# Small-block products of the gate and up projections: one weight row chunk at a time in place of two, with the raw rows released one chunk sooner

## The chip, the cores and the metric

The kernel runs on one core of a Trainium2 chip, as one launch. The metric is the device time of that core in microseconds (us), as the median of several runs. The engines of the core are TensorE (PE; its weight loads are listed apart as PEld), VectorE (DVE), ScalarE (ACT), GpSimd (POOL) and SyncE (SP), which issues most of the DMAs.

## The reference

One layer of an encoder on 1024 tokens of width 1024 in float32. First a mixer (gated short convolution and neighbourhood attention), then a mixture of experts, in which nearly all of the time studied here is spent:

```
logits = h @ w_router + b_router                     # 32 experts
top_v, top_i = top_k(logits, 4); gates = softmax(top_v)
# for each expert e, with xb the tokens that chose it:
g = minimum(xb @ w_gate[e] + b_gate[e], 7)
u = clip(xb @ w_up[e] + b_up[e], -7, 7)
y = (g * sigmoid(1.702 * g) * (u + 1)) @ w_down[e] + b_down[e]
out[token] += gate * y                               # plus the residual
```

w_gate, w_up and w_down are 1024 x 1024 float32 for each of 32 experts: 12 MB an expert, each read once from HBM.

## The kernel before

The expert part goes by passes. A pass serves one expert and up to 160 of its tokens: a main block of 128 tokens, and a small block of up to 32 more, which a pass has only if its expert was chosen by more than 128 tokens (flags `hb` for the pass whose down projection runs, `hbn` for the next pass, whose gate/up runs in the same trip of the loop).

The weights of a pass come in 12 chunks of 1 MB: 8 chunks of gate/up (chunk k holds row block k of w_gate and of w_up, 128 x 2048) and 4 of down (two row blocks each). SP loads them in order into `ring`, which has NSLOT = 6 slots; chunk c goes to slot c % 6. `room` (L463 and L464) lets SP load chunk c0 only when TensorE has finished chunk c0 - 6, which it learns from the semaphore `g_chunk` (one count for each chunk, given by the last product of the chunk). SP waits in order: a load that waits holds all later loads, the two bias loads among them (L455, L459).

For each chunk ScalarE makes w_hi, the weights rounded to a shorter float32 form (`round_weights`, L749), and VectorE makes w_lo, the raw weights minus w_hi (`rest_of_weights`, L1113). Both have six buffers. The main block's product is then three products with the 128 x 128 stationary operand x: w_hi with x_hi, w_lo with x_hi and w_hi with x_lo (`product`, L1491 to L1493), in the banks 0 to 3 of PSUM. A gate/up chunk has 4 x 3 = 12 such instructions of 512 columns.

The small block is multiplied in plain float32 straight from the raw rows in `ring` (L1502 for gate/up, L1537 for down). The output row of 1024 is cut into four quarters, and each quarter j is a product with a stationary operand of 128 x 32, whose result lies in the 32 partitions 32 j to 32 j + 31 of bank 6 (gate/up) or bank 7 (down). For one chunk k of gate/up these are four products of 512 columns, which the trace shows as 8 instructions, since a plain float32 product is two of them. The products of one or two chunks that stand together, ahead of the main products of a chunk, are called a group here.

In the loop, trip p runs on TensorE: `gate_up(p, 8, 0, ())` for chunk 0 of pass p + 1 with no small block, chunks 1 to 3 in a branch on `hbn` (`gate_up_first`), the transposes of the activations of pass p (`act_transpose`, L1525 and L1527), chunks 4 to 7 in a second branch (`gate_up_rest`), the bias rows (L1513, L1516), then the four chunks of down of pass p (`down_all`) with the transposes of pass p + 2's tokens (L1484) and its row numbers (L1474) between them, and the bias of down (L1549, L1551). The first gate/up, ahead of the loop, already does the small block chunk by chunk.

`extra_of(k, b)` says whose small-block products stand in chunk k: before, those of k - 1 and k in an odd chunk, none in an even one. So the raw rows of an even gate/up chunk are still read in the next chunk, and PAIRED lists the chunks of which `room` therefore asks for one count more. In its numbering 8, 10 and 12 are the gate/up chunks k = 0, 2 and 4 of the same trip, and 2 is k = 6 of the trip before. This holds for every pass, whether it has a small block or not, because SP's wait is the same in both.

Order on VectorE in a trip: w_lo of k = 0 and 1, the SwiGLU products of pass p (L1140 to L1145), w_lo of k = 2 and 3, slot numbers, w_lo of k = 4 and 5, aT_lo (L1150), w_lo of k = 6, 7 and of down 0 and 1, the reading of the gate and up results (`evacuate`, L1130 to L1135), w_lo of down 2 and 3, xT_lo (L1118), row numbers (L1095 to L1107).

Of the kernel before, what the change touches and what calls it, by code (L numbers as in the profile page):

```python
# [61 lines left out]
CH = 2048  # L62
NSLOT = 6
SPLIT = 6
PAIRED = (2, 8, 10, 12)
QD = 256
QT = 32
MSLOT = 4
# [44 lines left out]
def build(nc, A, out):  # L113
    ctx = ExitStack()
    with ctx:
# [252 lines left out]
        def hold(e, s, value):  # L368

            e.wait_ge(s, value)  # L370
            e.sem_inc(held, 1)
# [5 lines left out]
        def _(e):  # L377
# [83 lines left out]
            def room(p, c0):  # L461

                c = c0 - NSLOT  # L463
                hold(e, g_chunk, 12 * p + (c + 1 + (c in PAIRED)))  # L464
            e.wait_ge(e_mm, 2 * TT)
# [788 lines left out]
        def _(e):  # L1254
# [223 lines left out]
            def rows_transpose(n, first):  # L1478
                e.wait_ge(g_gat, 16 * n + 16)
                e.wait_ge(g_gatb, 16 * n + 16)  # L1480
                if not first:
                    e.wait_ge(g_ev, 2 * n)
                for k in range(KT):
                    e.transpose(bank[k // 4][:, P * (k % 4):P * (k % 4) + P], xg[:, P * k:P * k + P], ident[:, :])  # L1484
                for i in range(2):
                    ins = e.transpose(bank[2][:, P * i:P * i + P], xgb[:, P * i:P * i + P], ident[:, :])
                ins.then_inc(g_xtr, 1)
# [64 lines left out]

            def extra_of(k, b):

                return (k - 1, k) if b and k % 2 else ()
            rows_transpose(0, True)
            e.wait_ge(table_ok, 1)
            n_loop = e.value_load(table[0:1, 2 * NT:2 * NT + 1], min_val=1, max_val=MAX_PASSES)
# [18 lines left out]
            with e.Fori(0, n_loop) as p:  # L1577
# [8 lines left out]
                def gate_up_first(b):  # L1586
                    for k in range(1, 4):
                        gate_up(p, 8 + k, k, extra_of(k, b))

                def gate_up_rest(b):  # L1590
                    for k in range(4, GU_CHUNKS):
                        gate_up(p, 8 + k, k, extra_of(k, b))
                    gate_up_bias(p + 1, b)
# [55 lines left out]
```

## Time and profile before

| what | value |
|---|---|
| median of 3 runs | 2400.2 us (2400.07 to 2400.8) |
| the profiled execution, its own time | 2398.68 us |
| its span, first to last instruction | 2396.6 us |
| mean granted TensorE clock | 0.985 of full speed |
| PE busy | 2304.0 us, 96% of the span, 11110 instructions |
| PE weight loads busy | 1478.2 us, 62% |
| DVE busy | 1446.0 us, 60% |
| ACT busy | 1040.0 us, 43% |
| POOL busy | 912.5 us, 38% |
| HBM read / written | 468.34 MB / 32.05 MB |

The expert part runs from about 885 us to the end. In a line of grouped instructions the columns are: line of the kernel, engine, operation, output<-inputs, shapes, count, then busy time and mean ns of one, then idle time of the engine ahead of them with what ended it. In a timeline the first number is the start and the second the length, both in us; a bracket gives the idle time of the engine before it and what ended it ("issue" where the profile shows nothing that was waited for). A matmul's length includes the time its result takes to come out, so consecutive matmuls overlap in the rows: the distance of the starts is what one costs.

### The profile page before, as it was taken

The numbers are of one execution on the slowest core, as the hardware profiler recorded it, in microseconds if no ns is written. First come the engines' busy times: TensorE is split into PE (matmuls) and PEld (weight loads), VectorE is DVE, ScalarE is ACT, GpSimd is POOL, SyncE is SP. The second block draws the span as 40 slices with busy tenths as digits, with TensorE's granted clock in tenths as the row PEclk, the third lists the DMA queues.
The fourth block names the chain that finished last, engine by engine and source line by source line (L and its number), as shares of the span: only waits on it lengthen the run. The fifth ranks groups of instructions, "written<-read, shape, count | busy, mean of one in ns | idle before, by whom it ended". The sixth has DMA issues, their size and how long they took to land.

```text
span 2396.6 us, 34708 instructions
## 1 busy us (share of the span) xinstructions
PE 2304.0 (96%) x11110; PEld 1478.2 (62%) x11111; DVE 1446.0 (60%) x1842; ACT 1040.0 (43%) x1036; POOL 912.5 (38%) x508
## 2 busy tenths in 40 slices
PE   8999999999999967999999999999999999999996
PEld 4444444566665545777666666666676666666774
DVE  3123333421122356998877777787788777687885
ACT  2112222311010123666645555556466555565663
POOL 1123111000000016676554435644574564365573
PEclk9999999999999978999999999999999999999998
DMA  5412110021113245999988888898898888898994
GB/s 203 106 27 78 44 43 11 27 53 53 27 62 114 96 161 215 351 335 351 300 273 268 303 288 270 300 324 289 269 329 312 269 299 294 276 291 307 332 336 149
DMA packets 180051, 505.32 MB, mean 211 GB/s; under 512 B 18018, under 2 KB 60514, under 8 KB 180002
## 3 DMA queue, kind: packets, MB, share of 16 engines
q1 hardware_dynamic: 163874, 457.97, 54.1%
q0 software_dynamic: 16128, 46.67, 8.8%
q8 instruction: 33, 0.54, 0.1%
q14 instruction: 16, 0.13, 0.0%
HBM read 468.34 MB, written 32.05 MB: 209 GB/s over the span
## 4 chain that ended last, share of the span: by engine, by line
PE 84%; DVE 7%; issue 4%; DVEq 1%; ACT 1%; DMA 1%; POOL 0%; SPq 0%; ACTq 0%; POOLq 0%
PE psum L1491 13%; PE psum L1493 12%; PE psum L1492 12%; PE psum L1346 7%; PE psum L1290 7%; PE psum L1502 5%; PE psum L1378 4%; PE psum L1440 4%; DVE w_lo L1113 3%; PE psum L1389 2%; PE psum L1388 2%; PE psum L1390 2%; PE psum L1537 2%; PE psum L1516 1%; PE psum L1527 1%
## 5 line engine op out<-in xcount | busy, mean ns | idle before, releaser
L1113 DVE TENSOR_TENSOR w_lo<-ring,w_hi 128x2048 fp32r<-128x2048 f32 x384 | 874.2, 2307 | 68.2 <-ACT w_hi L749 54.6
L749 ACT ACTIVATE w_hi<-ring 128x2048 fp32r<-128x2048 f32 x384 | 721.3, 1919 | 157.5 <-DMA ring<-in_w_down 95.6
L589 POOL TENSOR_SCALAR pick<-iota_bf,slot_col 128x256 bf16<-128x256 bf16 x264 | 512.2, 1953 | 62.8 <-DVE slot_col L1126 62.8
L1491 PE MATMUL psum<-w_hi,xT_hi 128*128 128x512 f32 x1024 | 423.6, 414 | 40.1 <-DVE w_lo L1113 30.1
L1493 PE MATMUL psum<-w_hi,xT_lo 128*128 128x512 f32 x1024 | 406.9, 397 | 0.0
L1492 PE MATMUL psum<-w_lo,xT_hi 128*128 128x512 f32 x1024 | 406.5, 397 | 0.0
L595 POOL DMA_INDIRECT xg<-h_rows,idx_new x33 | 83.5, 2531 | 562.0 <-issue 535.8
L1491 PEld LDWEIGHTS psum<-w_hi,xT_hi 128*128 128x128 f32 x1024 | 193.4, 189 | 160.9 <-issue 69.1
L1493 PEld LDWEIGHTS psum<-w_hi,xT_lo 128*128 128x128 f32 x1024 | 193.6, 189 | 46.8
L1492 PEld LDWEIGHTS psum<-w_lo,xT_hi 128*128 128x128 f32 x1024 | 194.0, 189 | 40.3 <-issue 0.7
L1491 PE MATMUL psum<-w_hi,aT_hi 128*128 128x512 f32 x512 | 214.5, 419 | 3.4 <-DVE aT_lo L1150 3.4
L1493 PE MATMUL psum<-w_hi,aT_lo 128*128 128x512 f32 x512 | 203.7, 398 | 0.0
L1492 PE MATMUL psum<-w_lo,aT_hi 128*128 128x512 f32 x512 | 203.1, 397 | 0.0
L1346 PE MATMUL psum<-hT,ring 128*128 128x512 f32 x384 | 182.0, 609 | 0.0
L571 POOL TENSOR_TENSOR rstd<-var,half 128x1 f32<-128x1 f32 x8 | 4.4, 553 | 459.7 <-DVE var L1060 459.7
L1290 PE MATMUL psum<-ring,hT 128*128 128x512 f32 x384 | 168.4, 593 | 0.0
L998 DVE TENSOR_TENSOR ring<-psum,ring 128x512 f32<-128x512 f32 x32 | 22.1, 692 | 226.9 <-ACT ring L726 226.9
L1491 PEld LDWEIGHTS psum<-w_hi,aT_hi 128*128 128x128 f32 x512 | 96.7, 189 | 53.7 <-issue 34.9
L726 ACT ACTIVATE ring<-psum 128x512 f32<-128x512 f32 x32 | 19.1, 598 | 248.5 <-PE psum L1390 248.5
L1290 PEld LDWEIGHTS psum<-ring,hT 128*128 128x128 f32 x384 | 71.5, 191 | 81.9 <-issue 81.8
L1346 PEld LDWEIGHTS psum<-hT,ring 128*128 128x128 f32 x384 | 67.6, 189 | 83.5 <-issue 83.5
L1502 PE MATMUL psum<-ring,xTb 128*32 128x512 f32 x960 | 115.4, 598 | 0.0
(247 smaller groups left out, 2863.3 us busy)
## 6 DMA issues: line engine op xcount, KB each, us to landing
ring<-in_w_gate SPq DMA_DIRECT2D x256, 512.0 KB, 5.4
ring<-in_w_up SPq DMA_DIRECT2D x256, 512.0 KB, 6.4
ring<-in_w_down SPq DMA_DIRECT2D x256, 512.0 KB, 5.6
ring<-in_w_in SPq DMA_DIRECT2D x28, 512.0 KB, 5.2
ring<-in_x SPq DMA_DIRECT2D x16, 512.0 KB, 4.2
ring<-in_w_in SPq DMA_DIRECT2D x6, 1024.0 KB, 8.1
vb<-oT SPq DMA_DIRECT2D x16, 256.0 KB, 11.0
ring<-in_w_o SPq DMA_DIRECT2D x4, 1024.0 KB, 6.0
```

The source lines that it names most:

```text
L589: e.tensor_scalar(pick[:, t, :], iota_bf[:, :], slot_col[:, t, :], None, ALU.is_equal).then_inc(g_pick, 1)
L595: e.indirect_dma_start(out=xg[:, :], out_offset=None, in_=h2_rows, in_offset=bass.IndirectOffsetOnAxis(ap=idx_new[:, 0:1], axis=0)).then_i ...
L749: e.activation(w_hi[:, hs, :], ring[:, slot, :], ACT.Copy).then_inc(g_hi, 1)
L1113: e.tensor_tensor(w_lo[:, hs, :], ring[:, slot, :], w_hi[:, hs, :].bitcast(F32), ALU.subtract).then_inc(g_lo, 1)
L1290: ins = e.matmul(bank[n % 2][:, :], hT[:, k, P * t:P * t + P], item_view(2 * g + k // 4, 0, 4, 512)[:, k % 4, :], start=(k == 0), stop=(k ...
L1346: ins = e.matmul(bank[m % 2][:, :], wv[:, k, :], hT[:, k, 512 * hf:512 * hf + 512], start=(k == 0), stop=(k == KT - 1))
L1378: ins = e.matmul(bank[b0 + 2 + g][:, :], item_view(IT_MERGE + 2 * d + 1, 512 * g, 4, P)[:, k, :], src[:, k, cols], start=(k == 0), stop=(k ...
L1440: ins = e.matmul(bank[2 * (t % 2) + i][:, :], mixedT[:, k, P * t:P * t + P], item_view(IT_WO + k // 2, 0, 2, D)[:, k % 2, 512 * i:512 * i ...
L1491: e.matmul(dst, hi, w_up, start=start, stop=False)
L1492: e.matmul(dst, hi, w_rest, start=False, stop=False)
L1493: return e.matmul(dst, lo, w_up, start=False, stop=stop)
L1502: e.matmul(bank[6][QT * j:QT * j + QT, :].rearrange("p (g n) -> p g n", g=2), xTb[:, kb % 2, QT * (kb // 2):QT * (kb // 2) + QT], pair[:, ...
```

## The change

Two edits. `extra_of` gives chunk 1 the small-block products of chunks 0 and 1 as before, and every later chunk its own alone. PAIRED keeps only chunk 8 (k = 0), so SP may load the slots of k = 2, 4 and 6 as soon as TensorE has finished that chunk, not the next one.

```diff
-PAIRED = (2, 8, 10, 12)
+PAIRED = (8,)
```

```diff
             def extra_of(k, b):
 
-                return (k - 1, k) if b and k % 2 else ()
+                return () if not b else (0, 1) if k == 1 else (k,)
```

No instruction is added or removed on any engine but for the constants of SP's waits. Down's small block is untouched, and so is the first gate/up, which calls `gate_up` with (k,) itself.

## Rows read from the trace of the kernel before

**Rows 1.** The page's engine line and its chain that ended last.

```profile
PE 2304.0 (96%) x11110; PEld 1478.2 (62%) x11111; DVE 1446.0 (60%) x1842; ACT 1040.0 (43%) x1036; POOL 912.5 (38%) x508
...
PE 84%; DVE 7%; issue 4%; DVEq 1%; ACT 1%; DMA 1%; POOL 0%; SPq 0%; ACTq 0%; POOLq 0%
```

**Rows 2.** Stretches of one loop trip: length, busy per engine, PEclk, DMA share, GB/s.

```profile
1189.20:1241.20 52.00, 51.55 (x323) 32.91 (x322) 38.77 (x41) 28.10 (x24) 25.97 (x13) 1.00 0.84 279
1344.30:1389.00 44.70, 43.54 (x259) 31.41 (x256) 36.64 (x38) 27.59 (x23) 28.94 (x13) 1.00 0.91 311
1020.60:1061.00 40.40, 38.88 (x185) 29.33 (x185) 36.50 (x36) 27.12 (x22) 26.96 (x13) 1.00 1.00 345
```

**Rows 3.** Waits from 900 to 2390 us: total, times, longest.

```profile
ACT w_hi L749 <- DMA ring<-in_w_down: 95.6, 70, 3.5
ACT w_hi L749 <- DMA ring<-in_w_up: 56.6, 41, 15.6
...
PE psum L1491 <- DVE w_lo L1113: 30.1, 31, 6.8
```

**Rows 4.** The small block's products by count, and those of its bias row.

```profile
L1502 PE MATMUL psum<-ring,xTb 128*32 128x512 f32 x960 | 115.4, 598 | 0.0
...
L1513 PE MATMUL psum<-brow_gu,ones_bf 3*32 3x512 bf16 x60 | 5.9, 385 | 0.0
```

**Rows 5.** Timeline of PE, chunks k = 2 and 3 of one pass.

```profile
1540.62 0.40 PE L1491 MATMUL psum<-w_hi,xT_hi 128*128 128x512 f32 x1
...
1542.74 0.39 PE L1491 MATMUL psum<-w_hi,xT_hi 128*128 128x512 f32 x1
...
1543.52 1.92 PE L1502 MATMUL psum<-ring,xTb 128*32 128x512 f32 x16
1545.38 0.50 PE L1491 MATMUL psum<-w_hi,xT_hi 128*128 128x512 f32 x1
...
1546.18 0.39 PE L1491 MATMUL psum<-w_hi,xT_hi 128*128 128x512 f32 x1
```

**Rows 6.** Timeline of PE around a group of the down projection.

```profile
1517.79 0.40 PE L1491 MATMUL psum<-w_hi,aT_hi 128*128 128x512 f32 x1
...
1518.58 1.07 PE L1537 MATMUL psum<-ring,aTb 128*32 128x256 f32 x16
1519.59 0.50 PE L1491 MATMUL psum<-w_hi,aT_hi 128*128 128x512 f32 x1
...
1520.39 0.39 PE L1491 MATMUL psum<-w_hi,aT_hi 128*128 128x512 f32 x1
```

**Rows 7.** Timeline of the weight loads inside a group and behind it.

```profile
1535.85 0.16 PEld L1502 LDWEIGHTS psum<-ring,xTb 128*32 128x32 f32 x8 [0.37 <-issue]
...
1536.31 0.13 PEld L1502 LDWEIGHTS psum<-ring,xTb 128*32 128x32 f32 x4 [0.30 <-issue]
1536.74 0.13 PEld L1502 LDWEIGHTS psum<-ring,xTb 128*32 128x32 f32 x4 [0.30 <-issue]
...
1537.71 0.19 PEld L1491 LDWEIGHTS psum<-w_hi,xT_hi 128*128 128x128 f32 x1 [0.84 <-issue]
```

**Rows 8.** A pass with no small block: VectorE and TensorE around chunk k = 2.

```profile
1025.38 1.23 DVE L1145 SCALAR_TENSOR_TENSOR ut<-ut,st 128x1024 f32<-128x1024 f32 x1 [0.35 <-DVE st L1141]
1026.52 4.49 DVE L1113 TENSOR_TENSOR w_lo<-ring,w_hi 128x2048 fp32r<-128x2048 f32 x2
1028.86 0.51 PE L1491 MATMUL psum<-w_hi,xT_hi 128*128 128x512 f32 x1 [1.09 <-DVE w_lo L1113]
```

**Rows 9.** A pass with both small blocks: w_lo of k = 2 and 3, and TensorE's k = 2.

```profile
1195.61 4.49 DVE L1113 TENSOR_TENSOR w_lo<-ring,w_hi 128x2048 fp32r<-128x2048 f32 x2
...
1197.99 0.45 PE L1491 MATMUL psum<-w_hi,xT_hi 128*128 128x512 f32 x1
```

**Rows 10.** The same pass later: w_lo of k = 6 on, TensorE's k = 6.

```profile
1210.34 7.08 DVE L1113 TENSOR_TENSOR w_lo<-ring,w_hi 128x2048 fp32r<-128x2048 f32 x3 [0.51 <-ACT w_hi L749]
...
1214.46 0.40 PE L1491 MATMUL psum<-w_hi,xT_hi 128*128 128x512 f32 x1
```

**Rows 11.** The longest wait of ScalarE for weights in that pass, and its reader's start.

```profile
1219.84 1.92 ACT L749 ACTIVATE w_hi<-ring 128x2048 fp32r<-128x2048 f32 x1 [2.91 <-DMA ring<-in_w_down]
...
1224.99 1.21 DVE L1135 TENSOR_SCALAR ut<-psum 128x1024 f32<-128x1024 f32 x1
1226.13 2.28 DVE L1113 TENSOR_TENSOR w_lo<-ring,w_hi 128x2048 fp32r<-128x2048 f32 x1
```

## What the change was predicted to do

> **What bounds the kernel now.** I read the page first: TensorE is busy for 96% of the span and holds 84% of the chain that ended last [rows 1]. That is an average, so next came the stretches of single trips of the loop. I cut the trace at the last instructions of the down projection (L1551) and got 32 passes of four lengths, which depend only on which small blocks they hold. A trip with both (gate/up of the next pass, down of this one) takes 52.0 us with PE busy 51.55; one with the down block alone 44.7, and one with none 40.4 with PE busy 38.88 [rows 2]. The granted clock is 1.00 in all three, the 2.4 GHz level. The DMA share goes the other way: 0.84 in the trip with both blocks, 1.00 in the one with none. So a trip with a small block is TensorE's alone, and one with none has DMAs that run all the time. The reader is to see here that the edit's two halves work in different places: the split of the products costs TensorE in the trips where it has no slack, and the sooner release helps DMAs mostly in the other trips.
>
> Then the waits. ScalarE waits 152 us in all for weights to land, in 111 places. TensorE waits for w_lo for only 30.1 us, in 31 places [rows 3]. The question for the gain is whether the second is caused by the first, so I looked at single places in the timelines. The largest kind is chunk k = 2 of a pass with no gate/up block: TensorE waits 1.09 us for a w_lo that VectorE started at 1026.52, right behind its own SwiGLU product, which started at 1025.38 and takes 1.23 us [rows 8]. Nothing there waited for ScalarE or a DMA: it is the order of work on VectorE. The other kind, 0.4 us at chunk 0, stands likewise behind VectorE's row numbers. And ScalarE's longest regular wait, 2.91 us for a down chunk, ends with w_hi done at 1221.76, while VectorE is ready for it only at 1226.13, behind `evacuate` [rows 11]. That wait has 4.4 us of cover.
>
> **The change, part by part.**
>
> *Products.* The number of small-block instructions stays: 960, and the bias row's 60 at 4 for each pass say that 15 passes have such a block [rows 4]. The first of them starts inside the loop, so all 15 go through the changed branches. Each has now four groups of 16 instructions, in chunks 1, 3, 5 and 7. The one in chunk 1 stays. The other three become six groups of 8, in chunks 2 to 7.
>
> What does a group cost? In a stream of main products nine of them take 1542.74 - 1540.62 = 2.12 us, so 0.235 each and 2.82 for the twelve of a chunk [rows 5]. From the start of chunk 2 to the first main product of chunk 3 it is 1545.38 - 1540.62 = 4.76, which leaves 1.94 for the group. The next three products take 0.80 in place of 0.705, another 0.10: the first product behind a group is slow too. A group costs 2.04 us. In it four quarters run side by side, one batch of four every 0.43 us [rows 7], so 4 batches = 1.71 us of streaming and about 0.33 of fixed cost: some 0.1 to get in, some 0.2 to get out.
>
> The down groups give the same by other rows: 1519.59 - 1517.79 - 0.705 = 1.10, and 0.80 in place of 0.705 behind it, so 1.19 us for 16 instructions of 256 columns [rows 6]. Half the columns saves 0.85 us, the other 0.34 is fixed. Two shapes give the same fixed cost, so I take it to hang on the change between 128 x 32 and 128 x 128 operands and not on what is inside. A new group has 8 instructions of 512 columns, the same streaming as 16 of 256: I take the 1.19 of the down group for it.
>
> Sum: 6 x 1.19 - 3 x 2.035 = 7.14 - 6.11 = 1.03 us for each pass with a block, and 15 x 1.03 = 15.5 us. Bounds for the 45 added groups, as the trace has none with 8 instructions: the exit alone, if entering is free, 0.21 each and 9.5 us; and 0.45 each, 20 us, if a short group also fails to cover what a long one covers (each weight-load burst within a group shows 0.30 of idle and the entry 0.37 [rows 7], so 0.1 more is what these rows could hide). A cost below the exit's is unlikely, since it shows unchanged at either length. I take 0.34, the value of both shapes.
>
> *Is any of it hidden?* Cover would be time in which TensorE waits for something that does not move with it. In a trip with a gate/up block there is next to none: 0.45 us of 52.0 [rows 2]. Behind it the waits at chunk 0 and at k = 2 follow VectorE's row numbers and `evacuate`, which start from TensorE's own results and so move with it. Nothing is hidden.
>
> *Does a moved group meet a new wait?* Every gate/up chunk waits for its w_lo first, and the small block's products now stand behind that wait in chunks 2, 4 and 6 as well. The tight one is k = 2 with both blocks: two w_lo take 4.49 from 1195.61 on, so the first ends near 1197.9 and TensorE starts at 1197.99 [rows 9]. Its arrival at chunk 2 is unchanged, as chunks 0 and 1 are. At k = 6 w_lo is done near 1212.7 (2.3 us after 1210.34) and TensorE comes at 1214.46, some 0.3 later than now with the change [rows 10]. No new wait; queued behind it would be the rest of TensorE's trip.
>
> *Release.* SP's waits for the slots of k = 2, 4 and 6 end one chunk sooner, 2.8 us in a pass without a block, 4 us in one with it. In SP's queue behind them stand the down loads 0 and 2, the bias load of down between them, and chunk 0 of the pass after. All 31 trips get this. ScalarE gets its chunks sooner, in places where its waits are covered [rows 11]. I cost it at nothing: the work that hides the loads is TensorE's own stream, 5 chunks ahead. If that cover were gone the 30.1 us of [rows 3] would be the most to gain.
>
> Profiled execution: 2398.68 + 15.5 = 2414.2. It stands 1.5 us under the median of the runs, so the median becomes 2400.2 + 15.5 = 2415.7 us.
>
> **The rivals.**
>
> *The release pays.* If TensorE's 30.1 us behind w_lo were owed to late weights after all, the change gives 30.1 back for 15.5: 2400.2 - 14.6 = 2385.6 us. For it speaks the DMA share of 1.00 in trips without blocks [rows 2] and 152 us of ScalarE's waits [rows 3]. Against it, w_lo of k = 2 starts right behind VectorE's own work [rows 8]. It decides as soon as more than 15.5 of the 30.1 us, about half, goes. Chance 0.05.
>
> *The weight loads hide the change of shape.* Then a split costs next to nothing and the time is 2400 to 2404. Among main products every weight load lies beside the product before it, since a product of 128 x 512 with its own load comes every 0.235 us [rows 5]. Behind a group it does not: the load starts at 1537.71, in the instant of its product, after 0.84 us of idle with no cause shown [rows 7]. The Trainium skill, "TensorE: Matmul & The Clock Gate", Part 2, says that TensorE pulls weight loads ahead of running matmuls; by that rule alone the sum would be 0. The row behind a group differs from it. "TensorEngine Tiling (Array Packing)", Key Properties, says that changing the tiling mode drains TensorE, which speaks against the change and for the price of the rows. Chance 0.08 for the hiding.
>
> *A short group costs more, or a wait appears.* If the margin of 0.1 us at k = 2 [rows 9] goes, or short groups lose more than the fixed 0.34, each pass loses some 0.4 to 0.6 us more: 15 x 0.5 = 7.5, and 2423 us. Chance 0.08.
>
> *The release does not come sooner.* SP's later waits could end no sooner than before if it is held by chunk 0's, which keeps its count. That changes nothing in the sum, since the release is costed at nothing, and has no chance of its own.
>
> **How the numbers follow.** Forecast 0.79, release pays 0.05, hidden 0.08, dearer 0.08. The forecast's own range is 2400.2 + 9.5 to 2400.2 + 20 = 2409.7 to 2420.2. I widen it to 2407 to 2422, which takes in part of the third rival and a gain of a few us from the release, and leaves out the other two. A measurement of this kernel can tell 0.2%, 4.8 us, from no change. Slower by more than that: the forecast and the dear case, 0.79 + 0.08 = 0.87, of which I move 0.01 to the middle for a forecast that is partly hidden: 0.86; within it: 0.09; faster: 0.05.
>
> **What would show it.** In the profile after: L1502 still 960 with the same mean; in a pass with a gate/up block, one group of 16 and six of 8, each of these six adding 1.19 us between main products (0.86 of it streaming); trips with both blocks near 53.0 us and trips without any at 40.4. ScalarE's waits for DMA fall while TensorE's 30.1 us stay. I am wrong if trips without blocks get shorter (the release pays), if a group of 8 costs about 1.02, half of a group of 16 (hidden), or if L1502 or L1491 show waits for w_lo at k = 2 (dearer).

## The result, and the profile after

The changed kernel takes 2414.25 us (median of 4 runs, 2413.77 to 2415.01) against 2400.14 us for the kernel before in the same session, a ratio of 1.0062 with a 95% interval of 1.005 to 1.0074: 14.1 us slower, where 15.5 were forecast (2415.7 us, range 2407 to 2422).

Lines of the page after, TensorE's and the small block's, then the DMA issues with their us to landing (5.4, 6.4 and 5.6 us before for the same three):

```profile
PE 2321.7 (96%) x11110; PEld 1474.0 (61%) x11111; DVE 1443.2 (60%) x1842; ACT 1037.4 (43%) x1036; POOL 915.1 (38%) x508
...
L1502 PE MATMUL psum<-ring,xTb 128*32 128x512 f32 x960 | 124.7, 603 | 0.0
...
ring<-in_w_gate SPq DMA_DIRECT2D x256, 512.0 KB, 3.9
ring<-in_w_up SPq DMA_DIRECT2D x256, 512.0 KB, 5.1
ring<-in_w_down SPq DMA_DIRECT2D x256, 512.0 KB, 6.1
```

The same instructions, 960 of them, keep TensorE busy 9.3 us longer by themselves than in [rows 4]. A group's length in the rows includes the time in which its last results come out, and there are now more groups: two of 8 have 2 x 1.06 us where one of 16 has 1.92.

The stretches of single trips after, which answer to [rows 2] (both blocks, down block alone, none):

```profile
1191.20:1244.20 53.00, 52.54 (x324) 32.57 (x324) 38.69 (x41) 27.89 (x24) 26.15 (x13) 1.00 0.80 271
1349.20:1393.90 44.70, 43.53 (x259) 31.41 (x256) 36.63 (x38) 27.73 (x23) 28.63 (x13) 1.00 0.89 311
1022.00:1062.40 40.40, 38.88 (x186) 29.35 (x186) 35.94 (x36) 26.89 (x22) 28.02 (x13) 1.00 0.99 346
```

The trip with both blocks is 1.0 us longer, the two without a gate/up block have the same length to 0.1 us. Cut at the same instruction in both traces, the 15 trips with a gate/up block grew by 0.91 to 1.01 us each, 14.6 us together. Single trips without one differ by up to 0.4 us, most by less than 0.05. The two spans differ by 15.6 us, as the one of after is also 1.4 us later at the first of these cuts, ahead of which no changed product runs. So much differs from run to run: two runs below whose work up to this cut is the same, that with LATER and pairs and the first with late threes, have it at 982.0 and 980.2 us.

TensorE's timeline after, chunks k = 4 and 5 of a pass, which answers to [rows 5]:

```profile
1160.85 1.06 PE L1502 MATMUL psum<-ring,xTb 128*32 128x512 f32 x8
1161.84 0.50 PE L1491 MATMUL psum<-w_hi,xT_hi 128*128 128x512 f32 x1
1162.65 0.39 PE L1491 MATMUL psum<-w_hi,xT_hi 128*128 128x512 f32 x1
...
1164.06 0.40 PE L1491 MATMUL psum<-w_hi,xT_hi 128*128 128x512 f32 x1
1164.85 1.07 PE L1502 MATMUL psum<-ring,xTb 128*32 128x512 f32 x8
1165.85 0.50 PE L1491 MATMUL psum<-w_hi,xT_hi 128*128 128x512 f32 x1
```

From one group's start to the next it is 4.00 us. Twelve main products are 2.82 of it, so a group of 8 costs 1.18 us; 1.19 had been taken for it from the down groups. The reader sees the same two marks as in [rows 5]: the first product behind a group has 0.50 in place of 0.39 or 0.40, and the next quarter comes 0.81 later in place of 0.70.

The waits after, from 900 us on, which answer to [rows 3]:

```profile
ACT w_hi L749 <- DMA ring<-in_w_up: 34.6, 23, 15.8
ACT w_hi L749 <- DMA ring<-in_w_down: 33.2, 60, 1.1
PE psum L1491 <- DVE w_lo L1113: 28.6, 31, 5.8
```

The sooner release does what it says: ScalarE waits 68 us for weights in place of 152, and no longer than 1.1 us for a down chunk in place of 3.5. TensorE's own wait, in 31 places again, goes from 30.1 to 28.6 us, of which 1.0 is the single longest wait, at the entry of the loop (6.8 before, 5.8 after), and 0.4 one trip without a block. Neither can be put down to the release: of the run with late threes and that with groups beside the bias, whose releases are the same, one has 6.8 us at the entry and one 5.8, and the trip has its usual 40.35 us in the next run too, which lacks the sooner release. Half the change brought the weights sooner to an engine that was not late.

### The profile page after: what moved, and what is told of

Read it like the earlier page. It is cut to its first block, busy times and chain, and to the rows that moved or that the text cites. A ratio compares the mean times of both kernels' runs of the same rounds, so it can differ in the third digit from the quotient of the medians.

```text
span 2412.2 us, 34802 instructions
## 1 busy us (share of the span) xinstructions
PE 2321.7 (96%) x11110; PEld 1474.0 (61%) x11111; DVE 1443.2 (60%) x1842; ACT 1037.4 (43%) x1036; POOL 915.1 (38%) x508
## 4 chain that ended last, share of the span: by engine, by line
PE 86%; DVE 7%; issue 3%; DVEq 1%; ACT 1%; POOL 0%; DMA 0%; ACTq 0%; SPq 0%; POOLq 0%
PE psum L1491 14%; PE psum L1493 12%; PE psum L1492 12%; PE psum L1346 7%; PE psum L1290 7%; PE psum L1502 5%; PE psum L1378 4%; PE psum L1440 4%; DVE w_lo L1113 3%; PE psum L1389 2%; PE psum L1388 2%; PE psum L1390 2%; PE psum L1537 2%; PE psum L1516 1%; PE psum L1527 1%
## 5 line engine op out<-in xcount | busy, mean ns | idle before, releaser
L1113 DVE TENSOR_TENSOR w_lo<-ring,w_hi 128x2048 fp32r<-128x2048 f32 x384 | 870.2, 2299 | 65.9 <-ACT w_hi L749 52.3
L1491 PE MATMUL psum<-w_hi,xT_hi 128*128 128x512 f32 x1024 | 427.7, 418 | 38.1 <-DVE w_lo L1113 28.6
L1502 PE MATMUL psum<-ring,xTb 128*32 128x512 f32 x960 | 124.7, 603 | 0.0
```

Of the source, the lines that this page charges most:

```text
L1113: e.tensor_tensor(w_lo[:, hs, :], ring[:, slot, :], w_hi[:, hs, :].bitcast(F32), ALU.subtract).then_inc(g_lo, 1)
L1491: e.matmul(dst, hi, w_up, start=start, stop=False)
L1502: e.matmul(bank[6][QT * j:QT * j + QT, :].rearrange("p (g n) -> p g n", g=2), xTb[:, kb % 2, QT * (kb // 2):QT * (kb // 2) + QT], pair[:, ...
```

## The experiments

The theory to test had two halves: a group has a fixed cost of about 0.33 us, whatever is in it, which comes from the change of the stationary operand's shape; and the sooner release is worth nothing, because the loads have cover. Times are compared with runs of the kernel before on the same chip (2400.5, 2399.2 and 2400.1 us in the three sessions).

### The split without the release

```diff
-                return (k - 1, k) if b and k % 2 else ()
+                return () if not b else (0, 1) if k == 1 else (k,)
```

> The split of the small-block products alone, with the slots of k = 2, 4 and 6 released as late as before. Theory (each added group costs TensorE 0.33 us, the release is worth nothing): 45 groups add 14 to 15.5 us, so 2414 to 2416 us, the same as the changed kernel within 2 us, and trips with both blocks 53.0 us long. Rival (the release gives something back that hides a dearer split): slower than the changed kernel by what the release gives, 5 us or more.

Measured: 2413.62 us, ratio 1.0058 (1.0043 to 1.0074), the same as the changed kernel within 1 us. ScalarE's waits for DMA are back at 156 us, TensorE's are 29.6 us:

```profile
ACT w_hi L749 <- DMA ring<-in_w_down: 97.5, 70, 3.5
ACT w_hi L749 <- DMA ring<-in_w_up: 58.5, 43, 15.5
...
PE psum L1491 <- DVE w_lo L1113: 29.6, 31, 6.8
```

So the whole loss is the split's, and the 88 us of ScalarE's waits that the release removes are worth nothing here.

### Every slot held one chunk longer

```diff
-                hold(e, g_chunk, 12 * p + (c + 1 + (c in PAIRED)))
+                hold(e, g_chunk, 12 * p + (c + 2))
```

> The changed kernel, but SP asks for every chunk one count more, so each slot is released one chunk later than the raw rows need. Theory: the loads have over one chunk of cover, so the time is that of the changed kernel within 3 us (2412 to 2418), with ScalarE's waits for DMA back at 150 us or more. Rival (the loads are close to the path): TensorE's waits for w_lo grow from 29 us to 50 us or more and the time goes over 2425 us, first in the trips without a small block, where the DMA share is 1.00.

Measured: 2435.55 us, ratio 1.015 (1.0135 to 1.0166), 21 us over the changed kernel. The theory's number missed, and the rival's came. The trips with both blocks are still 53.0 us long; those without a gate/up block grew by 0.3 to 2.3 us. ScalarE, VectorE and TensorE in one of them:

```profile
1119.93 1.92 ACT L749 ACTIVATE w_hi<-ring 128x2048 fp32r<-128x2048 f32 x1 [6.14 <-DMA ring<-in_w_up]
...
1121.88 2.29 DVE L1113 TENSOR_TENSOR w_lo<-ring,w_hi 128x2048 fp32r<-128x2048 f32 x1 [2.12 <-ACT w_hi L749]
1121.95 1.09 ACT L768 ACTIVATE aT_hi<-psum 128x512 fp32r<-128x512 f32 x2
...
1126.46 4.78 DVE L1113 TENSOR_TENSOR w_lo<-ring,w_hi 128x2048 fp32r<-128x2048 f32 x2 [1.08 <-ACT w_hi L749]
1128.80 0.50 PE L1491 MATMUL psum<-w_hi,xT_hi 128*128 128x512 f32 x1 [1.51 <-DVE w_lo L1113]
```

The late chunk is k = 5. Its w_hi waits 6.14 us, and it stands in ScalarE's queue ahead of aT_hi, which then holds back aT_lo and with it the w_lo of k = 6. In trips with a down block alone TensorE waits at k = 5 as well. The cover for the loads is less than one chunk (2.8 us) in the trips without a gate/up block, and there is more than one in the others. The release is worth nothing only from where it stood before; one chunk later is on the path. The two are not the same slots, though: the change releases three of twelve sooner, this run holds eleven of twelve longer than the changed kernel, and which of the eleven costs the 21 us was not tried one by one.

### Down products in two groups in place of four

```diff
-                    for k in (2 * c, 2 * c + 1):
+                    for k in (range(2 * c - 2, 2 * c + 2) if c % 2 else ()):
...
-                                     ring[:, slot, off + QD * j:off + QD * j + QD], start=(k == 0), stop=False)
+                                     ring[:, (c0 + k // 2 - c) % NSLOT, off + QD * j:off + QD * j + QD], start=(k == 0), stop=False)
...
-PAIRED = (2, 8, 10, 12)
+PAIRED = (2, 4, 6, 8, 10, 12)
```

> The kernel before, but the small block's down products stand in two groups of 32 instructions (chunks 1 and 3) in place of four of 16, and the slots of down 0 and 2 are released one chunk later. Theory (fixed cost of about 0.34 us a group, whatever is in it): 2 groups fewer in each of 15 passes save 15 x 0.68 = 10.2 us, 2390 us; trips with a down block alone go from 44.7 to 44.0 us. Rival (the fixed cost grows with the length of a group, or the later release exposes loads): no gain, 2398 us or more.

Measured: 2396.42 us, ratio 0.9985 (0.9976 to 0.9994), faster by 4 us and not by 10. A group of 32 in its timeline:

```profile
1330.77 0.40 PE L1491 MATMUL psum<-w_hi,aT_hi 128*128 128x512 f32 x1
1331.57 1.93 PE L1537 MATMUL psum<-ring,aTb 128*32 128x256 f32 x32
1333.43 0.51 PE L1491 MATMUL psum<-w_hi,aT_hi 128*128 128x512 f32 x1
1334.24 0.40 PE L1491 MATMUL psum<-w_hi,aT_hi 128*128 128x512 f32 x1
```

1333.43 - 1330.77 - 0.705 is 1.955, and 0.10 behind it: 2.06 us for 32 instructions of 256 columns, against twice 1.19. The fixed cost does not grow with the length. But a trip with both blocks gave 0.48 us and not 0.68. One of the two groups that went had stood behind the wide bias products (L1516), and the change from these to the main products costs something by itself, as this run shows where no group is left between them:

```profile
1225.53 1.03 PE L1516 MATMUL psum<-brow_gu,ones_bf 3*128 3x512 bf16 x4
1226.49 0.50 PE L1491 MATMUL psum<-w_hi,aT_hi 128*128 128x512 f32 x1
1226.83 0.39 PE L1492 MATMUL psum<-w_lo,aT_hi 128*128 128x512 f32 x1
```

The bias products follow each other every 0.216 us, but the first main product starts 0.30 behind the last of them. It has 0.50 here too, and the next comes 0.34 behind it in place of 0.235. From the last bias product to the second main one it is 0.64 us, and it was 1.65 with the group of 0.86 between them: 0.15 was saved there, not 0.34. The rest went where the run before shows it: the first four trips without any block are 40.8 to 41.9 us long, in place of 40.35 to 40.7, because slots come free later there too. The five trips of 44.7 us with a down block alone, forecast at 44.0, took 43.4 to 44.7, four of them with new waits of 0.2 to 1.0 us at k = 5 or 6.

### The same, and later counts only where there is a small block

SP reads the flags of the pass and waits for the later count in a branch; gate/up stays in pairs.

```diff
-PAIRED = (2, 8, 10, 12)
+LATER = {2: 1, 4: 1, 6: 1, 8: 1, 10: 1, 12: 1}
...
-                hold(e, g_chunk, 12 * p + (c + 1 + (c in PAIRED)))
+                hold(e, g_chunk, 12 * p + (c + 1))
+                if c in LATER and flags:
+                    with e.If(flags[0 if c >= 8 else 1 if c < 4 else 2] > 0):
+                        hold(e, g_chunk, 12 * p + (c + 1 + LATER[c]))
```

> Gate/up groups as in the kernel before (pairs), the down products merged into two groups of 32, and SP asks for the later count only where the pass of that chunk has a small block. Theory (the merged down run lost part of its gain because slots came free later in trips that have no small block): trips without a block go back to 40.35 us and trips with both keep 51.04 to 51.6, so 7 us are saved, 2393 us. Rival (SP's branches cost as much as they save, or the waits came from the merging itself): 2396 us or more, as in the merged down run.

Measured: 2392.52 us, ratio 0.9966 (0.9952 to 0.9979), as the theory had it. Consecutive trips without a block are at 40.35 us again, trips with both at 51.04 to 51.62. Five trips with a down block alone went from 44.7 to between 43.6 and 44.4 us: the wait at k = 2, of the kind of [rows 8] and 1.05 us in such trips, is down to 0.2, and part of the gain is lost again in waits of 0.3 to 1.0 us at k = 5 or 6. (The two that follow a trip with a gate/up block alone keep 1.6 us at k = 2.) 0.85 us of TensorE's work has moved behind the row numbers, which gives VectorE that much more time; that this is the cause is read from the order of the work and was not tried by itself.

### Three gate/up groups in place of four

The rest is as in the run before. In this kernel and the next two SP's later counts (LATER) are those that the longer groups need.

```diff
-                return (k - 1, k) if b and k % 2 else ()
+                return () if not b else {2: (0, 1, 2), 5: (3, 4, 5), 7: (6, 7)}.get(k, ())
```

> As the run before, with the gate/up products in three groups (chunks 0 to 2, 3 to 5, 6 and 7) in place of four. Theory (0.34 us for each group left out, loads still covered): trips with both blocks 50.7 us, another 5 us saved, 2388 us. Rival (three slots held at once leave too little cover for the load of chunk 6, which can start only after chunk 2): TensorE waits for w_lo in trips with a block and the gain is lost, 2395 us or more.

Measured: 2403.76 us, ratio 1.0019 (1.001 to 1.0028), a loss where the theory had 2388. Trips with a gate/up block alone gave the 0.34 us (46.26 for 46.6) where TensorE does not wait at chunk 0. In the seven trips with such a block in which it does, there is a new wait at k = 2. VectorE and TensorE in the first trip with both blocks (L1118 and L1150 are the lines L1113 and L1145 of before, L1507 is L1502):

```profile
1191.29 0.50 PE L1496 MATMUL psum<-w_hi,xT_hi 128*128 128x512 f32 x1 [1.19 <-DVE w_lo L1118]
...
1195.55 1.22 DVE L1150 SCALAR_TENSOR_TENSOR ut<-ut,st 128x1024 f32<-128x1024 f32 x1
...
1196.68 4.49 DVE L1118 TENSOR_TENSOR w_lo<-ring,w_hi 128x2048 fp32r<-128x2048 f32 x2
...
1199.02 2.78 PE L1507 MATMUL psum<-ring,xTb 128*32 128x512 f32 x24 [1.84 <-DVE w_lo L1118]
```

TensorE comes to k = 2 without the 2.04 us of the group that had stood in chunk 1, and waits 1.84 us for a w_lo behind VectorE's SwiGLU product. That is the margin of 0.1 us in [rows 9], seen from its other side: the group in chunk 1 was cover. The waits at k = 2 of the seven trips are 10.3 us together (0.3 to 1.85 each). The rival has a part in the loss too: behind each trip with a gate/up block alone, as in the first row, the wait at chunk 0 is 1.05 to 1.6 us in place of 0.45, by the way that the next run shows.

### Three groups that leave the first where it was, and groups beside the bias

```diff
-                return (k - 1, k) if b and k % 2 else ()
+                return () if not b else {1: (0, 1), 4: (2, 3, 4), 7: (5, 6, 7)}.get(k, ())
```

> As the run with pairs and SP's later counts only where there is a small block, but gate/up in three groups that leave the first where it was: chunks 0 and 1 in chunk 1, 2 to 4 in chunk 4, 5 to 7 in chunk 7. Theory (the threes run lost at k = 2, where TensorE came 1.9 us sooner and met VectorE still behind its SwiGLU work; a group costs 0.34 us fixed): no wait at k = 2 in trips with a gate/up block, 0.34 us less in each of 15 trips than the pairs run, 2387 to 2388 us. Rival (the threes run lost to late loads, since three slots are held at once): waits of TensorE again, 2395 us or more.

Measured: 2392.84 us, ratio 0.997 (0.9958 to 0.9983). Trips with a gate/up block have no wait at k = 2, so that reading of the threes run holds. But the gain over pairs did not come (2387 to 2388 us had been forecast), and the rival's mechanism shows beside it, in ScalarE's waits for the down chunks whose slots are held longer. The rows are from a trip with a gate/up block alone and the start of the next:

```profile
1167.92 1.91 ACT L754 ACTIVATE w_hi<-ring 128x2048 fp32r<-128x2048 f32 x1 [5.71 <-DMA ring<-in_w_down]
...
1173.53 2.29 DVE L1118 TENSOR_TENSOR w_lo<-ring,w_hi 128x2048 fp32r<-128x2048 f32 x1 [1.37 <-ACT w_hi L754]
1174.35 1.03 PE L1521 MATMUL psum<-brow_gu,ones_bf 3*128 3x512 bf16 x4
1175.74 1.22 DVE L1135 TENSOR_SCALAR gt<-psum 128x1024 f32<-128x1024 f32 x1
...
1184.35 1.92 ACT L754 ACTIVATE w_hi<-ring 128x2048 fp32r<-128x2048 f32 x1 [0.58 <-DMA ring<-in_w_up]
1187.62 4.55 DVE L1118 TENSOR_TENSOR w_lo<-ring,w_hi 128x2048 fp32r<-128x2048 f32 x2 [0.41 <-issue]
1189.97 0.50 PE L1496 MATMUL psum<-w_hi,xT_hi 128*128 128x512 f32 x1 [1.04 <-DVE w_lo L1118]
```

The wait at chunk 0 is 1.04 us where it was 0.45. It is not chunk 0's own load that is late: its w_hi is done at 1186.27, and VectorE comes to it only at 1187.62. The late one is the first down chunk, 5.71 us. It moves the w_lo of the down chunks back, and with them the reading of the gate and up results that stands behind them on VectorE (`evacuate`, here from L1135 on), which starts 1.39 us behind the first bias product (L1521, L1516 of before) in place of 0.64 in the pairs run. All of VectorE's work up to w_lo of chunk 0 follows it. In every trip with a gate/up block alone the next wait at chunk 0 is as long as this delay and 0.3 us more. Trips with both blocks take 50.7 us behind another such trip (51.04 with pairs), and 51.9 to 53.8 behind a trip with a gate/up block alone (51.6).

The last run moves the last gate/up group and the last down group of this kernel behind the main products of their chunks, beside the narrow bias products:

```diff
-                for kb in extra:
+                if extra and k < GU_CHUNKS - 1:
+                    small(extra)
...
+                if extra and k == GU_CHUNKS - 1:
+                    ins = small(extra)
                 ins.then_inc(g_chunk, 1)
```

> As the run before, but the last gate/up group and the last down group stand behind the main products of their chunk, next to the narrow bias products. Theory (what costs is each change between 128 x 128 and 128 x 32 operands): two changes of shape and back less in a pass with a small block, up to 15 x 0.68 = 10 us less, 2377 to 2380 us. Rival (the cost is per group and not per change of shape): the same as the run before, 2387 us.

Measured: 2391.85 us, ratio 0.9968 (0.9956 to 0.998). Where no wait at chunk 0 stands ahead of them, trips with a gate/up block alone go from 46.27 to 46.06 us and those with both from 50.73 to 50.43: the sign is the theory's, the size 0.21 and 0.31 us in place of 0.34 and 0.68. The time of the whole is that of the run before within the runs' spread, as the rival had it. Part of what it gives goes into the wait at chunk 0, up to 1.55 us there.

### What the fixed cost hangs on

Three kernels with the changed kernel's groups, but other products in them. They make the small block's gate and up values meaningless and ran once each; only the distances from chunk to chunk are read, in stretches where the granted clock is 1.00 as in [rows 2].

```diff
-                    for j in range(4):
-                        e.matmul(bank[6][QT * j:QT * j + QT, :].rearrange("p (g n) -> p g n", g=2), xTb[:, kb % 2, QT * (kb // 2):QT * (kb // 2) + QT],
-                                 pair[:, :, QD * j:QD * j + QD], start=(kb == 0), stop=False)
+                    e.matmul(bank[6][:, :].rearrange("p (g n) -> p g n", g=2), xTb[:, kb % 2, :],
+                             pair[:, :, 0:QD], start=(kb == 0), stop=False)
```

> The changed kernel, but each group of gate/up is one plain float32 product of a 128 x 128 stationary operand with 512 columns (2 instructions) in place of four with 128 x 32 (8 instructions); the small block's gate and up values are therefore not the reference's. The streaming of a group is the same, 0.86 us. If the fixed cost hangs on the change between 128 x 128 and 128 x 32 operands, a group costs 0.86 to 0.95 us and the distance from chunk to chunk is 3.7 us; if it hangs on the change between rounded and plain float32, it stays at 1.18 us and 4.0 us.

The second and third replace the group by bfloat16 products of constants with routing rows:

```diff
+                    for j in range(4):
+                        e.matmul(bank[6][QT * j:QT * j + QT, :], ones_bf[:, QT * j:QT * j + QT], rows_bf[:, :, :, :].rearrange("p t e c -> p (t e c)")[:, 0:512], start=(kb == 0), stop=False)
```

> The changed kernel, but each quarter's product of the small block of gate/up is one bfloat16 product of 512 columns with a 128 x 32 stationary operand (constants and routing rows as operands), so a group has 4 instructions of 512 columns; the small block's gate and up values are not the reference's. Theory (the fixed cost of a group hangs on the change between 128 x 128 and 128 x 32, whatever the type): streaming 0.21 us and 0.33 us fixed, so the distance from chunk to chunk is 2.82 + 0.55 = 3.37 us. Rival (it hangs on plain float32 in narrow form): 3.03 us.

```diff
+                    e.matmul(bank[6][:, :], ones_bf[:, :], rows_bf[:, :, :, :].rearrange("p t e c -> p (t e c)")[:, 0:512], start=(kb == 0), stop=False)
```

> As the run before, but with one bfloat16 product of a 128 x 128 stationary operand in each group in place of four narrow ones; the small block's gate and up values are not the reference's. Theory: no fixed cost without a change of shape, 2.82 + 0.22 = 3.04 us from chunk to chunk. Rival (any foreign instruction between main products costs the 0.2 us at the exit): 3.2 us or more.

TensorE's timelines, two groups of each in this order: wide plain float32, narrow bfloat16, wide bfloat16. Ahead of the wide groups a row of the weight loads is shown too.

```profile
1161.70 0.42 PEld L1501 LDWEIGHTS psum<-ring,xTb 128*128 128x128 f32 x2
1161.94 1.02 PE L1501 MATMUL psum<-ring,xTb 128*128 128x512 f32 x2
...
1165.61 1.02 PE L1501 MATMUL psum<-ring,xTb 128*128 128x512 f32 x2
```

```profile
1163.80 0.40 PE L1502 MATMUL psum<-rows_bf,ones_bf 128*32 128x512 bf16 x4
1164.13 0.50 PE L1491 MATMUL psum<-w_hi,xT_hi 128*128 128x512 f32 x1
1164.94 0.39 PE L1491 MATMUL psum<-w_hi,xT_hi 128*128 128x512 f32 x1
...
1167.14 0.40 PE L1502 MATMUL psum<-rows_bf,ones_bf 128*32 128x512 bf16 x4
```

```profile
1161.05 0.10 PEld L1501 LDWEIGHTS psum<-rows_bf,ones_bf 128*128 128x128 bf16 x1 [0.27 <-issue]
1161.05 0.39 PE L1501 MATMUL psum<-rows_bf,ones_bf 128*128 128x512 bf16 x1
1161.10 0.59 PE L1491 MATMUL psum<-w_hi,xT_hi 128*128 128x512 f32 x1
1161.99 0.39 PE L1491 MATMUL psum<-w_hi,xT_hi 128*128 128x512 f32 x1
...
1164.10 0.39 PE L1501 MATMUL psum<-rows_bf,ones_bf 128*128 128x512 bf16 x1
```

Less the 2.82 us of the main products, a group costs:

| group | from chunk to chunk | cost | streaming | fixed |
|---|---|---|---|---|
| 8 narrow, float32 (the change) | 4.00 | 1.18 | 0.86 | 0.32 |
| 2 wide, float32 | 3.67 | 0.85 | 0.86 | 0 |
| 4 narrow, bfloat16 | 3.34 | 0.52 | 0.21 | 0.31 |
| 1 wide, bfloat16 | 3.05 | 0.23 | 0.21 | 0.02 |

The streaming is two steps of 0.43 us for float32 [rows 7] and, as an estimate, half a step for bfloat16: the bias products of 512 columns in bfloat16 (L1516) follow each other every 0.216 us. The three distances are within 0.03 us of what the theory expected. Only the narrow groups have the fixed cost, and in both types: it belongs to the change between 128 x 128 and 128 x 32 operands and not to the change of type or to a foreign instruction in the stream. What in that change takes the time, the shape of the operand or the place of the result in 32 of the partitions, these runs don't tell apart.

## Why the prediction was right, point by point

**The bound.** Right for the trips with a gate/up block, where next to nothing was hidden: each grew by 0.91 to 1.01 us. That a trip's length depends only on its blocks is not so. The trip before counts too, by the waits at chunk 0 and k = 2: before the change, trips with both blocks take 52.1 or 51.5 us, with a down block alone 44.7 or 46.0, without any 40.35 or 39.0. The sum does not rest on it.

**The price of a group.** Right: 1.19 us was taken for a group of a kind that the trace did not have, and 1.18 was measured. The fixed 0.34 held at 8, 16 and 32 instructions (0.32, 0.33 and 0.35).

**The sum.** 15.5 us were forecast and 14.1 measured; by trips, 1.03 was forecast and 0.97 measured on average. In the trips with both blocks that start with a wait of 0.45 us at chunk 0 the growth is only 0.91 to 0.94, against 0.98 in those that don't. There the first main product of k = 2 was 0.05 us late before (0.45 long in [rows 9]): from k = 2 to the first main product of k = 3 it was 4.80 us before and 4.75 in the other trips, and it is the same in both kinds now. Most of the difference is the price: at the measured 1.18 us a group the sum is 15 x 0.97 = 14.6 us, which is what the trips gave together. The 0.5 us from there to the median's 14.1 is within the spread of the runs.

**The hidden weight loads.** The rival fell in every run with a narrow group. Behind the changed kernel's groups TensorE's weight loads show again 0.84 us of idle:

```profile
1164.85 0.16 PEld L1502 LDWEIGHTS psum<-ring,xTb 128*32 128x32 f32 x8 [0.36 <-issue]
1165.85 0.19 PEld L1491 LDWEIGHTS psum<-w_hi,xT_hi 128*128 128x128 f32 x1 [0.84 <-issue]
```

Behind a wide group there is next to no fixed cost. The Trainium skill, "TensorEngine Tiling (Array Packing)", Key Properties, has the drain at a change of tiling mode, and the table above agrees with it so far as the cost is there with such a change and not without. The Trainium skill, "TensorE: Matmul & The Clock Gate", Part 2, has weight loads pulled ahead of running matmuls: the rows show it among the main products and ahead of the wide float32 ones (load at 1161.70, product at 1161.94), and not at a change to narrow operands or back. A late load in the rows is no proof of a cost, though: that of the wide bfloat16 product starts with its product too (1161.05), and that group costs its streaming alone.

**The release.** That it is worth nothing was right: the split alone takes the same time. The reason given was too broad. I called the cover TensorE's stream, 5 chunks ahead, and the step rested on one place with 4.4 us of cover, in a trip with a block [rows 11]. In trips without a gate/up block the cover at k = 5 is under one chunk, and holding the slots one chunk longer cost 21 us. Sooner and later are not alike: the release of three slots one chunk sooner gives 0, that of nearly all one chunk later costs 21 us.

**The new wait at k = 2.** Right that none appears, since TensorE's arrival there is unchanged. The threes run shows how near it was. At k = 6 TensorE was to come some 0.3 us later than before; four groups of 8 in place of two of 16 stand ahead of it, and it comes 0.7 later (0.7 is also what 4 x 1.19 - 2 x 2.035 gives). That only widens the margin there.

## A version that is faster than both

The kernel with pairs in gate/up, two down groups and SP's later counts only where there is a small block takes 2392.52 us, 0.34% under the kernel before, where the changed kernel is 0.62% over the kernel before. Two further steps in the same direction (fewer groups, groups beside the bias) came out at 2392.84 and 2391.85 us, which these runs don't tell from it. What each gains in changes of shape goes, for the most part, into TensorE's wait at chunk 0, behind down chunks whose slots come free later.

## What to carry to other kernels

Where TensorE sets the time, put products with narrow stationary operands into few, long groups: here each switch from the main products to 128 x 32 operands and back cost 0.31 to 0.35 us, whatever stood between. Before buying a sooner release with such switches, look whether the wait that it shortens ends in TensorE's: here 88 us of ScalarE's waits went and TensorE kept its own. And a group's place can be cover for another engine, so moving it can cost more than its switches.

## What the runs showed of the hardware that was not expected

A change of number format alone was next to free on TensorE: plain float32 and bfloat16 products of full width between rounded float32 ones cost 0.85 and 0.23 us, their streaming to within 0.02. And the cost of a change of shape shows only in part where another kind of product stands beside the group: one of two removed groups, with the bias products ahead of it, and the groups moved beside the narrow bias gave 0.1 to 0.25 us less than the 0.34 of the stream. For the first the rows give the reason: the change from stationary operands of 3 rows and 128 columns to those of 128 x 128 costs some 0.2 us by itself.
